# A routed expert layer: one loop for wide and narrow blocks, index products inside the down products

## The chip, the cores and the metric

The kernel runs on one core of a Trainium2 chip. The metric is the device time of one execution in microseconds (us). Engines: PE is TensorE (matrix products and transposes), DVE is VectorE, ACT is ScalarE, POOL is GpSimd, SP is SyncE. 16 DMA engines move data between the chip's memory (HBM) and the on-chip buffer.

## The reference

Two layers of a diffusion backbone over 512 latent and 256 context tokens of width 1024, in float32. Each layer has a mixer (recurrence and attention in the first, a state-space layer in the second) and then a routed mixture of 64 experts of hidden width 256 beside a shared one. Layer 0 routes all 768 tokens, layer 1 the 512 latent ones. What matters here is the expert part:

```python
def moe_ffn(h, router_w, router_bias, w_gate, w_up, w_down, ws_gate, ws_up, ws_down):
    affinity = jax.nn.sigmoid((h @ router_w).astype(f32))
    _, idx = lax.top_k(affinity + router_bias.astype(f32), TOP_K)      # TOP_K = 6
    ...
    def expert_block(acc, blk):
        tok, g, e = blk
        y = swiglu(h_ext[tok], w_gate[e], w_up[e], w_down[e])
        return acc.at[tok].add(y * g[:, None]), None
    ...
    return acc[:n_tok] + swiglu(h, ws_gate, ws_up, ws_down)
```

where `swiglu(x, g, u, d)` is `(silu(x @ g) * (x @ u)) @ d`. An expert's three matrices are 1 MB each (1024 x 256, 1024 x 256 and 256 x 1024).

## The kernel before

The program runs in order: preparation, mixer 0, the experts of layer 0, the state-space mixer, the experts of layer 1. An expert part is `moe_route` (router, ranks of the tokens, a table of work items), `moe_loop` and `moe_combine` (adds three accumulators in memory to the stream).

`moe_loop` is what changes. The tokens of an expert are cut into blocks. A **wide** block has up to 128 tokens on the 128 partitions. A **narrow** one has up to 64: each token lies as two half rows of 512 features on two partitions, and the products work on pairs of 64-column tiles. How many blocks of each kind there are is known only when the router has run, so each engine reads the counts from the table and walks loops of `UNROLL` = 6 unrolled bodies, each behind a branch (`items`, L1135 to L1140). First all wide blocks are done (`WIDE_TRIPS` trips of six: 72 counts in layer 0, 60 in layer 1), then all narrow ones (`NARROW_TRIPS`, 66 counts). A count beyond the number of blocks only costs the branch.

What a block takes, with its lines before the change:

- SP (`load`, L1148) reads the expert's number from the table, waits for `gu_mm` (gate and up products of the block whose ring slot is reused), issues the gate and up loads, waits for `y_mm` (that block's down products) and issues the down load. The wide ring has 2 slots, the narrow ring 3. SP works in order.
- DVE marks in `onehot` which tokens are in the block (`mark_wide`, `mark_narrow`), `AHEAD` = 4 blocks ahead. PE multiplies that with the table of ids and gates (`pick`, six small products in layer 0, L1340), DVE sums the result to indices and gates (`tokens`, L1289 to L1298), POOL gathers the rows (L1170, L1176).
- PE transposes the gathered rows into `pT` (L1347, L1353), ACT copies them to `xT`.
- PE multiplies gate and up (`up_wide` L1361, `up_narrow` L1372), ACT makes the silu (L1240, L1250), DVE the product `hid` (L1303, L1313), PE transposes it (L1383, L1404), DVE copies `hidT` (L1306, L1316), PE multiplies down (L1395, L1416), ACT copies the result with the gate as a scale (L1245, L1255), and POOL adds the rows to an accumulator in memory by an indirect DMA (L1186, L1196).

PE's order is written by hand: in the body of block i come gate and up of block i+1, then the hid transposes of i, the row transposes of i+2, `pick` of i+4, then the down products of i. So silu and product of a block lie beside other PE work. Each float32 product appears as two records.

## Time and profile before

| what | us |
|---|---|
| median of 3 runs | 3109.47 |
| lowest and highest of them | 3103.22, 3113.58 |
| the profiled execution | 3128.16 |
| its span, first to last instruction | 3126.4 |
| mean granted clock of PE, share of full speed | 0.857 |
| PE busy in the span | 2291.5 (73%) |
| weight loads of the experts, 3 x 138 of 1024 KB, median to landing | 10.2, 14.9, 13.1 |
| HBM read and written | 628.15 and 94.65 MB |

The first expert load of layer 0 is issued at 893.5 us, the last down product of its narrow blocks ends at 1779.4 and the combine begins at 1798.2. In layer 1 the same marks are 2345, 3075.7 and 3089.8. A DMA share is the mean busy share of the 16 DMA engines; q1 is SP's queue, q0 POOL's, which carries gathers and adds; the columns of a queue row are packets, MB and the time its packets took as a share of 16 engines over the window. A share can pass 1 a little where packets overlap. The number in brackets at the end of a timeline row is the idle time of that engine before the instruction and what ended it.

### The profile page before, as it was taken

The page shows a single profiled execution, that of the slowest core. Times are in us where ns is not written, and L with a number is a line of the kernel's source. Part 1 is how long each engine was busy: PE and PEld are TensorE (multiplying, and loading weights), DVE is VectorE, ACT ScalarE, POOL GpSimd, SP SyncE. Part 2 cuts the span into 40 slices and gives each one's busy share as a digit, 9 for nine tenths or more (in the row PEclk, how much of TensorE's full clock was granted, in tenths as well). Part 3 has the DMA queues.
Part 4 walks back from the last instruction along what each step waited for, and adds up shares of the span by engine and source line. Part 5 has one row for each costly group of instructions (what it writes and reads, how often), then busy time and mean ns, then how long its engine had stood idle before and what let it go on. Part 6 is the DMA issues. An engine that isn't in the chain of part 4 may idle for free. (4 is left out here: it accounts for less than half of the span.)

```text
span 3126.4 us, 40427 instructions
## 1 busy us (share of the span) xinstructions
PE 2291.5 (73%) x12118; PEld 1322.8 (42%) x12119; DVE 969.9 (31%) x2071; ACT 584.4 (19%) x964; POOL 566.7 (18%) x468
## 2 busy tenths in 40 slices
PE   3996996677758889887787606269776886777772
PEld 2884543443434444444444305265343443444441
DVE  4742256641411111111222147842231111111113
ACT  2232233420201111111111113021111111111110
POOL 2530000000011111122232231300002112222222
PEclk8998998969879999998999857558987898999986
DMA  9973101001337787788999575123136877999995
GB/s 321 337 261 114 54 27 67 1 1 56 157 141 251 262 283 245 275 274 323 397 387 376 208 250 167 32 91 114 44 128 237 277 240 284 395 375 367 383 380 170
DMA packets 183539, 684.02 MB, mean 219 GB/s; under 512 B 34234, under 2 KB 36730, under 8 KB 145082
## 3 DMA queue, kind: packets, MB, share of 16 engines
q1 hardware_dynamic: 136042, 581.86, 49.7%
q0 software_dynamic: 38784, 71.13, 9.6%
q10 hardware_dynamic: 8624, 29.82, 2.4%
q8 instruction: 58, 0.95, 0.1%
q14 instruction: 31, 0.25, 0.0%
HBM read 628.15 MB, written 94.65 MB: 231 GB/s over the span
## 5 line engine op out<-in xcount | busy, mean ns | idle before, releaser
L1372 PE MATMUL pGU_m<-wgu_m,xT_m 128*64 128x256 f32 x2816 | 376.5, 428 | 158.9 <-DMA wgu_m<-in_exp_w_up 158.9
L1361 PE MATMUL pGU_m<-wgu_m,xT_m 128*128 128x512 f32 x800 | 401.2, 660 | 85.9 <-DMA wgu_m<-in_exp_w_up 85.9
L1372 PEld LDWEIGHTS pGU_m<-wgu_m,xT_m 128*64 128x64 f32 x2816 | 221.5, 154 | 348.3 <-DMA wgu_m<-in_exp_w_up 228.7
L1361 PEld LDWEIGHTS pGU_m<-wgu_m,xT_m 128*128 128x128 f32 x800 | 168.0, 213 | 314.3 <-issue 208.6
L1176 POOL DMA_INDIRECT xgn_m<-moe_h,idxn_m x96 | 99.8, 1040 | 500.2 <-DVE idxn_m L1295 472.9
L1395 PE MATMUL pY_m<-wd_m,hidT_m 128*128 128x512 f32 x400 | 186.9, 610 | 0.1
L1416 PE MATMUL pY_m<-wd_m,hidT_m 128*64 128x512 f32 x704 | 173.7, 612 | 4.0
L1316 DVE COPY hidT_m<-pHT_m 128x128 f32<-128x128 f32 x88 | 25.6, 291 | 433.9 <-PE pHT_m L1404 433.9
L1196 POOL DMA_INDIRECT moe_acc<-yn_m,idxn_m x88 | 140.0, 1591 | 108.0 <-ACT yn_m L1255 99.9
L1231 ACT ACTIVATE xT_m<-pT_m 128x1024 f32<-128x1024 f32 x54 | 55.2, 1023 | 531.0 <-PE pT_m L1347 531.0
L1234 ACT ACTIVATE xT_m<-pT_m 128x512 f32<-128x512 f32 x92 | 54.9, 597 | 529.3 <-PE pT_m L1353 529.3
L819 POOL MEMSET zero_r<- 128x1024 f32 x2 | 1.9, 951 | 794.7 <-POOLq L69 523.7
L1170 POOL DMA_INDIRECT xgw_m<-moe_h,idxw_m x58 | 60.0, 1035 | 465.2 <-DVE idxw_m L1298 457.0
L1306 DVE COPY hidT_m<-pHT_m 128x256 f32<-128x256 f32 x50 | 21.2, 424 | 393.4 <-PE pHT_m L1383 393.4
L1283 DVE TENSOR_TENSOR onehot_m<-iota_slot_l,rank_l 128x512 bf16 (+1 forms) x96 | 77.6, 809 | 181.5 <-issue 181.5
L579 PE MATMUL ps_a<-W_a,hT_a 128*128 128x512 f32 x288 | 124.1, 592 | 0.0
L2186 PE MATMUL ps_s<-UV_s,ZU_s 128*128 128x512 f32 x256 | 113.1, 605 | 0.7 <-ACT ZU_s L2006 0.7
L2155 PE MATMUL ps_s<-XS_s,Wb_s 128*128 128x64 f32 x256 | 54.8, 421 | 77.6 <-ACT XS_s L1996 77.6
L1186 POOL DMA_INDIRECT moe_acc<-yw_m,idxw_m x50 | 79.6, 1592 | 161.4 <-ACT yw_m L1245 161.4
L1395 PEld LDWEIGHTS pY_m<-wd_m,hidT_m 128*128 128x128 f32 x400 | 73.0, 192 | 73.6 <-issue 73.4
L1340 PE MATMUL pI_m<-pick_rhs_l,onehot_m 128*128 x776 | 50.8, 168 | 54.9 <-DVE onehot_m L1276 31.9
L1276 DVE TENSOR_TENSOR onehot_m<-iota_slot_l,rank_l 128x768 bf16 (+1 forms) x58 | 50.3, 866 | 123.8 <-issue 123.8
(375 smaller groups left out, 3394.3 us busy)
## 6 DMA issues: line engine op xcount, KB each, us to landing
wgu_m<-in_exp_w_gate SPq DMA_DIRECT2D x138, 1024.0 KB, 10.2
wgu_m<-in_exp_w_up SPq DMA_DIRECT2D x138, 1024.0 KB, 14.9
wd_m<-in_exp_w_down SPq DMA_DIRECT2D x138, 1024.0 KB, 13.1
w_p<-in_mod_w SPq DMA_DIRECT2D x24, 2048.0 KB, 14.5
acc_c<-moe_acc SPq DMA_DIRECT2D x30, 512.0 KB, 11.1
W_a<-in_ar_w_in SPq DMA_DIRECT2D x5, 2048.0 KB, 8.5
moe_acc<-zero_r ACTq DMA_DIRECT2D x20, 512.0 KB, 18.0
s_w<-Wt_p ACTq DMA_DIRECT2D x8, 1152.0 KB, 9.8
```

The source lines that it names most:

```text
L579: last = pe.matmul(bank(n % 4), hT[:, k, t * P:(t + 1) * P], W[:, c % 2, k, :], start=(k == 0), stop=(k == KD - 1))
L1170: pool.indirect_dma_start(xg_w[b % 3][:], None, h_dram, bass.IndirectOffsetOnAxis(idx[0][b][:].bitcast(U32), 0), bounds_check=last_row, oo ...
L1176: pool.indirect_dma_start(xg_n[b % 3][:], None, h_half, bass.IndirectOffsetOnAxis(idx[1][b][:].bitcast(U32), 0), bounds_check=last_half, o ...
L1186: pool.indirect_dma_start(accs[b % 2], bass.IndirectOffsetOnAxis(idx[0][b][:].bitcast(U32), 0), y_w[b % 2][:], None, bounds_check=last_row ...
L1196: pool.indirect_dma_start(acc_half[b % 3], bass.IndirectOffsetOnAxis(idx[1][b][:].bitcast(U32), 0), y_n[b % 3][:], None, bounds_check=last ...
L1231: act.activation(xT[b][:], pT[:].rearrange("p (k c) -> p k c", c=P), ACT.Copy).then_inc(W['xT_done'], 1)
L1283: dve.tensor_tensor(onehot[:].rearrange("p t (a s) -> p t a s", a=2), slots, rank[:, :, bass.ds(e, 1)].rearrange("p t (a o) -> p t a o", a ...
L1361: last = pe.matmul(pGU[b % 2][:], xT[b % 2][:, k, :], wgu[b % WIDE_RING][:, :, k, :], start=(k == 0), stop=(k == KD - 1))
L1372: last = pe.matmul(pGU[b % 2][H * side:H * side + H, 0, :].rearrange("p (j n) -> p j n", j=2), narrow_xT[b % 2][:, k % 4, H * (k // 4):H * ...
L1395: last = pe.matmul(pY[:, half * 512:(half + 1) * 512], hidT[:, k, :], wd[b % WIDE_RING][:, k, half * 512:(half + 1) * 512], start=(k == 0) ...
L1416: last = pe.matmul(pY[H * side:H * side + H, (b % 2) * 512:(b % 2 + 1) * 512], hidT[:, 0, H * k:H * k + H], w[:, k, side * 512:(side + 1) ...
L2186: last = pe.matmul(ps[:, (2 * (u % 4) + half) * 512:(2 * (u % 4) + half + 1) * 512], zT[:, k, m * P:(m + 1) * P], glu[:, k, c:c + 512], st ...
```

## The change

- The two loops become one (`trips`). Each of its `TRIPS` (12 in layer 0, 11 in layer 1, six counts each) takes, per count i, up to four steps, each behind its own branch: wide gate and up of i, narrow gate and up of i, the rest of wide i, the rest of narrow i. When the wide blocks are used up, the narrow ones go on alone.
- SP issues the gate and up loads of both kinds, then the down loads of both kinds.
- PE's `pick` moves from before the down products to between their halves. The wide row transposes are split in two halves of four, with one bank of `pT_w`, and a half stands on either side of the first half of the down products. Gate and up of block i now stand in the body of block i itself.
- DVE's `mark` moves behind `tokens` and works one block further ahead, with a `onehot` of each kind. At the end of each rest PE waits for `idx_done`.
- Wide and narrow have their own tiles: one `pGU_w` bank, `pGU_n` with two halves, `hid`, `hidT`, `xT`, `pY` of each kind, and a shared bank for `pHT` and `pI`. `y_n` has 2 buffers instead of 3.
- Wide adds go to accumulator 0 alone, each after the one before has landed; narrow adds alternate between accumulators 1 and 2.
- Wide down weights are loaded as one row of 8 KB for each partition instead of two of 4 KB, and `hid`'s columns are transposed in the order that fits. Narrow down weights stay as they are.
- The prologue fills both kinds alternately. ACT follows the order silu wide, silu narrow, rest wide, rest narrow.

```diff
-    WIDE_TRIPS = -(-most_wide // UNROLL)
-    NARROW_TRIPS = -(-NE // UNROLL)
-    assert max(most_wide, NE) + AHEAD <= ROWS
+    TRIPS = -(-max(most_wide, NE) // UNROLL)
+    assert max(most_wide, NE) + AHEAD + 1 <= ROWS
...
-        def items(eng, n, trips, body):
-
-            with eng.Fori(0, trips) as q:
+        def trips(eng, n_wide, n_narrow, steps):
+
+            with eng.Fori(0, TRIPS) as q:
                 for b in range(UNROLL):
-                    with eng.If(n > q * UNROLL + b):
-                        body(q * UNROLL + b, q, b)
...
+                    i = q * UNROLL + b
+                    for kind, step in steps:
+                        with eng.If((n_narrow if kind else n_wide) > i):
+                            step(i, q, b)
 
         @block.sync
         def _(sp):
-            def load(kind, i, q, b):
-                ring = (WIDE_RING, NARROW_RING)[kind]
-                slot = b % ring
-                to = slot + WIDE_RING * kind
+            def gate_up(kind, i, b):
+                slot = b % (WIDE_RING, NARROW_RING)[kind]
                 e = expert(sp, kind, i)
                 sp.wait_ge(S[kind]['gu_mm'], i + 1)
                 for j, w in enumerate((w_gate, w_up)):
-                    sp.dma_start(wgu[to][:, j], w[bass.ds(e, 1)].rearrange("e (p k) n -> p (e k) n", k=KD))\
+                    sp.dma_start(wgu[kind][slot][:, j], w[bass.ds(e, 1)].rearrange("e (p k) n -> p (e k) n", k=KD))\
                       .then_inc(gu_loaded[kind][slot], 16)
+
+            def down(kind, i, b):
+                slot = b % (WIDE_RING, NARROW_RING)[kind]
+                e = expert(sp, kind, i)
                 sp.wait_ge(S[kind]['y_mm'], i + 1)
-                sp.dma_start(wd[to][:], w_down[bass.ds(e, 1)].rearrange("e (k p) n -> p (e k) n", p=P))\
+                rows = ("e (p k) n -> p (e k) n", "e (k p) n -> p (e k) n")[kind]
+                sp.dma_start(wd[kind][slot][:], w_down[bass.ds(e, 1)].rearrange(rows, k=2))\
                   .then_inc(d_loaded[kind][slot], 16)
-            items(sp, count(sp, 0), WIDE_TRIPS, lambda i, q, b: load(0, i, q, b))
-            items(sp, count(sp, 1), NARROW_TRIPS, lambda i, q, b: load(1, i, q, b))
+
+            trips(sp, count(sp, 0), count(sp, 1),
+                  ((0, lambda i, q, b: gate_up(0, i, b)), (1, lambda i, q, b: gate_up(1, i, b)),
+                   (0, lambda i, q, b: down(0, i, b)), (1, lambda i, q, b: down(1, i, b))))
...
             def wide(i, q, b):
                 pool.wait_ge(W['idx_done'], i + AHEAD + 1)
-                pool.wait_ge(W['xT_mm'], i + 2)
+                pool.wait_ge(W['xT_mm'], i * 2 + 4)
                 gather_wide((b + AHEAD) % UNROLL)
                 pool.wait_ge(W['y_done'], i + 2)
+                pool.wait_ge(yw_added, i * 16 + 32)
                 pool.sem_inc(W['pool_go'], 1)
-                pool.indirect_dma_start(accs[b % 2], bass.IndirectOffsetOnAxis(idx[0][b][:].bitcast(U32), 0),
+                pool.indirect_dma_start(accs[0], bass.IndirectOffsetOnAxis(idx[0][b][:].bitcast(U32), 0),
                                         y_w[b % 2][:], None, bounds_check=last_row, oob_is_err=False,
-                                        compute_op=ALU.add).then_inc(y_added[b % 2], 16)
+                                        compute_op=ALU.add).then_inc(yw_added, 16)
...
+            def rest_wide(i, q, b):
+                for half in range(2):
+                    act.wait_ge(W['xT_mm'], i * 2 + 5 + half)
+                    evac_wide(b, half)
+                act.wait_ge(W['y_mm'], i + 1 + WIDE_RING)
+                act.wait_ge(yw_added, i * 16 + 16)
+                act.activation(y_w[b % 2][:], pY_w[:], ACT.Copy, scale=gslot[0][b][:]).then_inc(W['y_done'], 1)
...
+            def gated_wide(i, q, b):
                 dve.wait_ge(W['silu_done'], i + 1)
-                dve.tensor_tensor(hid[:], hsil[:], pGU[b % 2][:, 1, :], ALU.mult).then_inc(W['hid_done'], 1)
+                dve.tensor_tensor(hid_w[:], hsil_w[:], pGU_w[:, 1, :], ALU.mult).then_inc(W['hid_done'], 1)
                 dve.wait_ge(W['hidT_mm'], i + 1)
                 dve.wait_ge(W['y_mm'], i + WIDE_RING)
-                dve.tensor_copy(hidT[:], pHT[:]).then_inc(W['hidT_done'], 1)
-                dve.wait_ge(y_added[b % 2], q * 48 + 16 * (b // 2) + 16)
+                dve.tensor_copy(hidT_w[:], pHT).then_inc(W['hidT_done'], 1)
+
+            def gated_narrow(i, q, b):
+                dve.wait_ge(N['silu_done'], i + 1)
+                dve.tensor_tensor(hid_n[:], hsil_n[:], pGU_n[:, b % 2, 1, :], ALU.mult).then_inc(N['hid_done'], 1)
+
+            def rest_wide(i, q, b):
+                dve.wait_ge(yw_added, i * 16 + 16)
                 tokens(0, i + AHEAD, (b + AHEAD) % UNROLL)
-
-            def narrow(i, q, b):
-                mark_narrow(i + AHEAD)
-                dve.wait_ge(N['silu_done'], i + 1)
-                dve.tensor_tensor(hid[:, 0:P], hsil[:, 0:P], pGU[b % 2][:, 0, P:2 * P], ALU.mult).then_inc(N['hid_done'], 1)
+                mark_wide(i + (AHEAD + 1))
+
+            def rest_narrow(i, q, b):
                 dve.wait_ge(N['hidT_mm'], i + 1)
                 dve.wait_ge(N['y_mm'], i + NARROW_RING)
-                dve.tensor_copy(hidT[:, 0], pHT[:, 0]).then_inc(N['hidT_done'], 1)
-                dve.wait_ge(y_added[(b + 1) % 3], wide_adds(nw, (b + 1) % 3) * 16 + q * 32 + 16 * ((b + 1) // 3) + 16)
+                dve.tensor_copy(hidT_n[:], pHT[:, 0, :]).then_inc(N['hidT_done'], 1)
+                dve.wait_ge(yn_added[b % 2], q * (16 * UNROLL // 2) + 16 * (b // 2) + 16)
                 tokens(1, i + AHEAD, (b + AHEAD) % UNROLL)
+                mark_narrow(i + (AHEAD + 1))
...
-            def wide(i, q, b):
-                with pe.If(n_wide > q * UNROLL + (b + 1)):
-                    up_wide((b + 1) % UNROLL, i + 2, q * (32 * UNROLL // WIDE_RING) + 32 * ((b + 1) // WIDE_RING + 1), i + 1)
+            def rest_wide(i, q, b):
                 pe.wait_ge(W['hid_done'], i + 2)
-                pe.wait_ge(W['hidT_done'], i + 1)
                 for k in range(2):
-                    last = pe.transpose(pHT[:, k, :], hid[:, k * P:(k + 1) * P], ident[:])
+                    last = pe.transpose(pHT[:, k, :], hid_w[:].rearrange("p (c k) -> p k c", k=2)[:, k, :], ident[:])
                 last.then_inc(W['hidT_mm'], 1)
                 pe.wait_ge(gathered[0][(b + 2) % 3], q * (16 * UNROLL // 3) + 16 * ((b + 2) // 3 + 1))
-                pe.wait_ge(W['xT_done'], i + 2)
-                rows_wide((b + 2) % UNROLL)
-                pe.wait_ge(W['idx_done'], i + AHEAD)
-                pick(0, i + AHEAD)
-                pe.wait_ge(W['hidT_done'], i + 2)
+                pe.wait_ge(W['xT_done'], i * 2 + 4)
+                rows_wide((b + 2) % UNROLL, 0)
+                pe.wait_ge(W['hidT_done'], i + 1)
                 pe.wait_ge(d_loaded[0][b % WIDE_RING], q * (16 * UNROLL // WIDE_RING) + 16 * (b // WIDE_RING + 1))
                 pe.wait_ge(W['y_done'], i + 1)
                 for half in range(2):
                     for k in range(2):
-                        last = pe.matmul(pY[:, half * 512:(half + 1) * 512], hidT[:, k, :],
-                                         wd[b % WIDE_RING][:, k, half * 512:(half + 1) * 512], start=(k == 0), stop=(k == 1))
+                        last = pe.matmul(pY_w[:, half * 512:(half + 1) * 512], hidT_w[:, k, :],
+                                         wd[0][b % WIDE_RING][:, k, half * 512:(half + 1) * 512], start=(k == 0), stop=(k == 1))
+                    if half == 0:
+                        pick(0, i + AHEAD)
+                        pe.wait_ge(W['xT_done'], i * 2 + 5)
+                        rows_wide((b + 2) % UNROLL, 1)
                 last.then_inc(W['y_mm'], 1)
-
-            def narrow(i, q, b):
-                with pe.If(n_narrow > q * UNROLL + (b + 1)):
-                    up_narrow((b + 1) % UNROLL, i + 2, q * (32 * UNROLL // NARROW_RING) + 32 * ((b + 1) // NARROW_RING + 1), i + 1)
+                pe.wait_ge(W['idx_done'], i + AHEAD + 1)
+
+            def rest_narrow(i, q, b):
                 pe.wait_ge(N['hid_done'], i + 2)
+                pe.transpose(pHT[:, 0, :], hid_n[:], ident[:]).then_inc(N['hidT_mm'], 1)
+                pe.wait_ge(gathered[1][(b + 2) % 3], q * (16 * UNROLL // 3) + 16 * ((b + 2) // 3 + 1))
+                pe.wait_ge(N['xT_done'], i + 2)
+                rows_narrow((b + 2) % UNROLL)
                 pe.wait_ge(N['hidT_done'], i + 1)
-                pe.transpose(pHT[:, 0, :], hid[:, 0:P], ident[:]).then_inc(N['hidT_mm'], 1)
-                pe.wait_ge(gathered[1][(b + 2) % 3], q * (16 * UNROLL // 3) + 16 * ((b + 2) // 3 + 1))
-                pe.wait_ge(N['xT_done'], i + 1)
-                rows_narrow((b + 2) % UNROLL)
-                pe.wait_ge(N['idx_done'], i + AHEAD)
-                pick(1, i + AHEAD)
-                pe.wait_ge(N['hidT_done'], i + 2)
                 pe.wait_ge(d_loaded[1][b % NARROW_RING], q * (16 * UNROLL // NARROW_RING) + 16 * (b // NARROW_RING + 1))
                 pe.wait_ge(N['y_done'], i + 1)
-                w = wd[WIDE_RING + b % NARROW_RING]
+                w = wd[1][b % NARROW_RING]
                 for k in range(2):
                     for side in range(2):
-                        last = pe.matmul(pY[H * side:H * side + H, (b % 2) * 512:(b % 2 + 1) * 512],
-                                         hidT[:, 0, H * k:H * k + H], w[:, k, side * 512:(side + 1) * 512],
-                                         start=(k == 0), stop=(k == 1))
+                        last = pe.matmul(pY_n[H * side:H * side + H, :], hidT_n[:, H * k:H * k + H],
+                                         w[:, k, side * 512:(side + 1) * 512], start=(k == 0), stop=(k == 1))
+                    if k == 0:
+                        pick(1, i + AHEAD)
                 last.then_inc(N['y_mm'], 1)
+                pe.wait_ge(N['idx_done'], i + AHEAD + 1)
...
+            trips(pe, n_wide, n_narrow, ((0, up_wide), (1, up_narrow), (0, rest_wide), (1, rest_narrow)))
```

Three places show the new order.

**SP, one trip's loads.** `wgu`, `wd` are the gate and up and the down weights; w and n at a name's end are wide and narrow. Before, in either loop:

```order
L1139 COMPARE_AND_BRANCH
...
L1133 TENSOR_LOAD table_l
...
L1155 DMA wgu_m<-in_exp_w_gate 128x2048
L1155 DMA wgu_m<-in_exp_w_up 128x2048
L1158 DMA wd_m<-in_exp_w_down 128x2x1024
```

and now, without the branch and the register load ahead of each pair:

```order
L1151 DMA wguw_m<-in_exp_w_gate 128x2048
L1151 DMA wguw_m<-in_exp_w_up 128x2048
...
L1151 DMA wgun_m<-in_exp_w_gate 128x2048
L1151 DMA wgun_m<-in_exp_w_up 128x2048
...
L1159 DMA wdw_m<-in_exp_w_down 128x2048
...
L1159 DMA wdn_m<-in_exp_w_down 128x2x1024
```

The gate and up loads of the narrow block moved ahead of the wide block's down load.

**PE, a wide body.** `pGU` holds gate and up, `pHT` (in `pHI` now) the transposed hidden values, `pT` the transposed rows, `pI` (in `pHI` now) the index products, `pY` the down products. Before:

```order
L1361 MATMUL pGU_m<-wgu_m,xT_m 128x512 x8
...
L1383 MATMUL pHT_m<-ident_l,hid_m 128x128 x2
...
L1347 MATMUL pT_m<-ident_l,xgw_m 128x128 x8
...
L1340 MATMUL pI_m<-pick_rhs_l,onehot_m 128x5
...
L1395 MATMUL pY_m<-wd_m,hidT_m 128x512 x4
```

and now one merged trip, up to the narrow transposes:

```order
L1369 MATMUL pGUw_m<-wguw_m,xTw_m 128x512 x8
...
L1380 MATMUL pGUn_m<-wgun_m,xTn_m 64x256 x16
...
L1388 MATMUL pHI_m<-ident_l,hidw_m 128x128 x2
...
L1355 MATMUL pTw_m<-ident_l,xgw_m 128x128 x4
...
L1398 MATMUL pYw_m<-wdw_m,hidTw_m 128x512 x2
...
L1348 MATMUL pHI_m<-pick_rhs_l,onehotw_m 128x5
...
L1355 MATMUL pTw_m<-ident_l,xgw_m 128x128 x4
L1398 MATMUL pYw_m<-wdw_m,hidTw_m 128x512 x2
...
L1409 MATMUL pHI_m<-ident_l,hidn_m 128x128
```

Between the hid transposes and the first down product stand four row transposes where eight and the index products stood.

**DVE, from the wide hid copy on.** Before, a wide body:

```order
L1276 TENSOR_TENSOR onehot_m<-iota_slot_l,rank_l 128x768
...
L1303 TENSOR_TENSOR hid_m<-hsil_m,pGU_m 128x256
...
L1306 COPY hidT_m<-pHT_m 128x256
...
L1290 TENSOR_REDUCE gslotw_m<-pI_m 128x1
L1291 TENSOR_REDUCE idf_m<-pI_m 128x1
L1298 TENSOR_SCALAR idxw_m<-idf_m 128x1
```

and now, wide and narrow:

```order
L1310 COPY hidTw_m<-pHI_m 128x256
...
L1314 TENSOR_TENSOR hidn_m<-hsiln_m,pGUn_m 128x128
...
L1295 TENSOR_REDUCE gslotw_m<-pHI_m 128x1
L1296 TENSOR_REDUCE idfw_m<-pHI_m 128x1
L1303 TENSOR_SCALAR idxw_m<-idfw_m 128x1
...
L1281 TENSOR_TENSOR onehotw_m<-iota_slot_l,rank_l 128x768
...
L1324 COPY hidTn_m<-pHI_m 128x128
```

The wide `onehot` and its register loads now stand ahead of the narrow `hidT` copy.

## Rows read from the trace of the kernel before

**Rows 1.** Page, part 2: GB/s of the DMA engines in 40 slices.
```profile
GB/s 321 337 261 114 54 27 67 1 1 56 157 141 251 262 283 245 275 274 323 397 387 376 208 250 167 32 91 114 44 128 237 277 240 284 395 375 367 383 380 170
```

**Rows 2.** Windows: us; busy PE, PEld, DVE, ACT, POOL; clock, DMA, GB/s.
```profile
930.00:1420.00 490.00, 428.31 (x1342) 208.66 (x1340) 72.90 (x200) 79.91 (x100) 86.46 (x66) 0.93 0.78 259
...
1480.00:1750.00 270.00, 209.06 (x1512) 114.30 (x1513) 57.54 (x180) 43.82 (x90) 79.09 (x60) 0.93 1.02 387
...
1779.40:1798.20 18.80, 0.03 (x1) 0.00 (x0) 0.00 (x0) 0.69 (x1) 1.59 (x1) 0.50 0.03 3
...
3075.70:3089.80 14.10, 0.00 (x0) 0.00 (x0) 0.00 (x0) 0.69 (x1) 1.59 (x1) 0.61 0.14 25
```

**Rows 3.** DMA queues, layer 0: wide 930 to 1420, narrow 1480 to 1750.
```profile
q1 hardware_dynamic: 18144, 102.37, 57.2%
...
q0 software_dynamic: 9250, 24.49, 20.7%
...
q1 hardware_dynamic: 17081, 95.68, 88.2%
...
q0 software_dynamic: 6637, 8.68, 13.4%
```

**Rows 4.** DMA queues, layer 1: wide 2380 to 2595, narrow 2660 to 3040.
```profile
q1 hardware_dynamic: 7840, 44.04, 56.1%
...
q0 software_dynamic: 4032, 8.79, 17.3%
...
q1 hardware_dynamic: 23669, 133.06, 87.6%
...
q0 software_dynamic: 9258, 11.39, 12.6%
```

**Rows 5.** Timeline, two wide blocks on PE: start, us, instruction, idle before.
```profile
1109.69 8.57 PE L1361 MATMUL pGU_m<-wgu_m,xT_m 128*128 128x512 f32 x16 [3.75 <-DMA wgu_m<-in_exp_w_up]
...
1118.32 1.13 PE L1347 MATMUL pT_m<-ident_l,xgw_m 128*128 128x128 f32 x8
...
1130.04 1.12 PE L1347 MATMUL pT_m<-ident_l,xgw_m 128*128 128x128 f32 x8
...
1131.15 3.68 PE L1395 MATMUL pY_m<-wd_m,hidT_m 128*128 128x512 f32 x8
```

**Rows 6.** Timeline, the row transposes of two narrow blocks on PE.
```profile
1455.24 0.65 PE L1353 MATMUL pT_m<-ident_l,xgn_m 128*128 128x128 f32 x4
...
1461.55 0.65 PE L1353 MATMUL pT_m<-ident_l,xgn_m 128*128 128x128 f32 x4
```

**Rows 7.** Timeline, DVE between two wide blocks.
```profile
1119.61 0.16 DVE L1290 TENSOR_REDUCE gslotw_m<-pI_m 128x1 f32<-128x3 f32 x1 [0.58 <-PE pI_m L1340]
...
1119.94 0.15 DVE L1298 TENSOR_SCALAR idxw_m<-idf_m 128x1 int32<-128x1 f32 x1
...
1121.67 0.96 DVE L1276 TENSOR_TENSOR onehot_m<-iota_slot_l,rank_l 128x768 bf16 x1 [1.58 <-issue]
```

**Rows 8.** Waits of the SyncE queue, 930 to 1420: total us, times, longest.
```profile
SPq L1158 <- PE pY_m L1395: 385.6, 32, 16.6
```

**Rows 9.** Lines, ACT, 900:1435, 1435:2000, 2374:2609, 2600:3126: xcount, busy, mean ns.
```profile
L1245 ACT ACTIVATE yw_m<-pY_m,gslotw_m 128x1024 f32<-128x1024 f32 x34 | 37.9, 1113 | 96.4 <-PE pY_m L1395 96.4
...
L1255 ACT ACTIVATE yn_m<-pY_m,gslotn_m 128x512 f32<-128x512 f32 x38 | 26.1, 687 | 66.4 <-PE pY_m L1416 66.4
...
L1240 ACT ACTIVATE hsil_m<-pGU_m 128x256 f32<-128x256 f32 x16 | 6.0, 375 | 6.7 <-PE pGU_m L1361 6.7
...
L1255 ACT ACTIVATE yn_m<-pY_m,gslotn_m 128x512 f32<-128x512 f32 x50 | 34.4, 687 | 83.9 <-PE pY_m L1416 83.9
```

**Rows 10.** Timeline, ACT: silu after each layer's first gate and up.
```profile
934.53 0.38 ACT L1240 ACTIVATE hsil_m<-pGU_m 128x256 f32<-128x256 f32 x1 [6.79 <-PE pGU_m L1361]
...
2381.90 0.38 ACT L1240 ACTIVATE hsil_m<-pGU_m 128x256 f32<-128x256 f32 x1 [6.68 <-PE pGU_m L1361]
```

**Rows 11.** Source L1139, the loop's branch on PE, 1781 to 1799.
```profile
L1139 PEldq COMPARE_BRANCH  x16: 208/208/208, 1781.0 to 1787.3; - x16
```

196 lines of the change are left out of this document (88 added, 108 removed).

## The prediction

> **What bounds the kernel now.** I read the slices of the page first [rows 1]. In the expert loop of layer 0 the DMA engines move 245 to 283 GB/s for about 500 us and then close to 390; layer 1 repeats this (237 to 284, then about 380). So each loop has two stages with different limits. The windows say which [rows 2]. In the wide stage (930 to 1420) PE is busy 428 of 490 us and the DMA share is 0.78. In the narrow stage (1480 to 1750) the DMA share is 1.02 and PE is busy 209 of 270 us. The first wants PE, the second wants DMA, and they run one after the other.
>
> The price of a block comes from the queue rows [rows 3, 4]. Three weight tiles are 3.146 MB, so 102.37 MB on q1 are 32.5 wide blocks in 490 us, 15.1 us each; 95.68 MB are 30.4 narrow blocks in 270 us, 8.9 us each. In layer 1: 14.0 in 215 us (15.4 each), 42.3 in 380 us (9.0 each). One wide and one narrow block cost 24.0 us one after the other in layer 0, 24.3 in layer 1.
>
> Why does a wide block take 15.1 us? From one set of row transposes to the next is 11.72 us where PE did not wait [rows 5]. The block before waited 3.75 us for weights and then needed 8.57 us for its gate and up products; the same in the undisturbed block is part of the 11.72. SyncE explains the wait: its queue stood 385.6 us of the stage before the load of the down weights, until PE was done with an older down product [rows 8], and the next gate and up loads stand behind that in order. Undisturbed, a narrow block takes 6.31 us of PE [rows 6].
>
> **The two resources of a merged trip.** DMA: I add the time shares of both queues at each kind's own price. Layer 0: wide (57.2% + 20.7%) x 490 / 32.5 = 11.74 us, narrow (88.2% + 13.4%) x 270 / 30.4 = 9.02 us. The saturated stage reaches a sum of 1.016, so a pair needs 20.76 / 1.016 = 20.4 us. Layer 1: 11.27 + 9.00 = 20.3, by its own sum of 1.00 20.2 us. The other bound is by bytes: 6.29 MB of weights, 0.754 MB of wide and 0.286 MB of narrow gathers and adds, 7.33 MB at the narrow stage's 387 GB/s, 18.9 us. I take the queue time, since a packet of the wide stage's gathers and adds was measured at its own duration, and keep 18.9 as the low end.
>
> The saturated row moved 387 GB/s. The Trainium skill, page "DMA: Bandwidth & Descriptors", section Specifications, gives a limit of about 358 GB/s of HBM for a core. The row is above it; by the page the 7.33 MB would take an estimated 20.5 us, by the row 18.9.
>
> PE: 11.72 + 6.31 = 18.0 us of work, plus three new exposures in the order. (a) The wide hidT copy is covered by four row transposes instead of eight and the index products: 0 to 0.5 us, I take 0.2. (b) In the narrow rest the hidT copy on DVE stands behind the wide index sums (0.48 us from the first to the last [rows 7]) and the wide onehot, which needs 1.58 us of register loads and 0.96 us of work; PE covers it by half the row transposes (0.56) and half the down product (1.84 [rows 5]) plus its own narrow transposes (0.65 [rows 6]): 0 to 1 us, I take 0.5. (c) After the narrow down product PE's sequencer waits for the narrow indices, with only the second half of that product queued behind it: 0.2 to 0.8 us, I take 0.5. Queued behind this wait is the next trip's whole gate and up product. Together 19.2 us, ends 18.2 to 20.3. PE is just under DMA, so I forecast DMA-bound trips of **20.4 and 20.2 us**.
>
> **Is DMA fed?** The moved loads on SyncE decide it. Now the gate and up loads of both kinds are issued once the wide product two trips back is done, and a down load no longer holds up its own kind's next gate and up load. When PE waits for a wide gate tile, behind it are queued the narrow one, two down tiles and the whole next trip, about 10 MB or 25 us. The queue does not run dry. The four loads a trip need four register loads and branches, hidden in 20 us. The single accumulator for wide adds makes each add wait for the one before, one trip of 20 us earlier; the narrow adds keep two. No cost.
>
> **Rows of 8 KB** change 128 descriptors of a wide down load. The 2 KB rows of the page's third slice reach 337 GB/s, the mixed 4 and 8 KB rows of the narrow stage 397 [rows 1]: 0.45 us per MB at most between them, so at most 0.2 us a wide block, at least 0. Within the rounding; 0 taken. The new hidden-column order costs no instruction.
>
> **Counts** are 34 wide and 38 narrow in layer 0, 16 and 50 in layer 1 [rows 9]. So 34 and 16 merged trips, then 4 and 34 trips with a narrow block alone. There, gate and up, silu, product and transposes stand in a row, where before the next block's product lay between. I estimate 1 to 2 us on top of 6.31 (the wide silu alone is 375 ns [rows 9]), so 7.3 to 8.3 us, still under the 8.9 to 9.0 of DMA: nothing taken, up to 1 us a trip kept for the range.
>
> **The end of the loop** gets dearer. 72 and 66 counts of the unrolled loop are walked whatever the blocks, and each now has four branches on PE. After layer 0's last narrow block 34 counts are left: 136 branches instead of 28. The rows show 16 of them in 6.3 us, 0.42 us each [rows 11]; part of that is loop and counter work that isn't multiplied, so 0.31 to 0.42, I take 0.37: 50 us, starting 3.7 us before the last product ends. Before, the combine began 18.8 us after it [rows 2]; now it would be 46.5: **28 us lost**. Layer 1: 64 branches, 24 us, about 21 against 14.1: **7 us lost**. The jump between the stages (38 and 44 branches) goes, but DMA was full there, so no gain counts.
>
> That branch took 208 ns itself. The Trainium skill, page "Advanced Engine Details and Errata", section Control Flow Timing, gives about 108 ns for compare-and-branch. The row is twice that; by the page the 136 branches would be an estimated 15 us, hidden before the combine, and both losses would be nil.
>
> **The sum.** Two pairs fit in the rings and load during the index work. The third pair's load starts when the first wide product ends: 934.5 and 2381.9 [rows 10]. Layer 0: 934.5 + 32 x 20.4 + 4 x 8.9 + 2 for the last down product = 1625, against 1779.4 before, 154 less; after the branches 126. Layer 1: 2381.9 + 14 x 20.2 + 34 x 9.0 + 2 = 2973 against 3075.7, 103 less; after the branches 96. Together 222 us. The profiled execution took 3128.2 us (span 3126.4), so 2906 in its terms; the median of the runs is 3109.5, so **2887**.
>
> **The rivals.** (1) *PE is the bound, and dearer than I think.* For it: PE is within 1.2 us of DMA, several waits now stand in one trip, and a wait for weights already cost 1.5 us in slower products. Against: the ends of the exposures sum to 20.3 only. At 22 us a trip: 32 x 1.6 + 14 x 1.8 = 76 more, 2963; with 1 us more for each of 38 narrow trips 3001. (2) *DMA is cheaper,* by bytes, and PE at 19.2 us is the floor: 32 x 1.2 + 14 x 1.0 = 52 less, 2835; with branches at 0.31 another 12 less, 2823. (3) *The clock turns it slower.* The granted clock is 0.93 in both stages [rows 2]; after a wait of 3.75 us the products took 8.57 us [rows 5]. If every piece of a merged trip, cut up by waits, ran at 1.2 instead of 2.4 GHz, PE would need up to 36 us. It decides from 222 / 46 = 4.8 us above my trip, 25.2 us, that is a third of PE's 18 us at the lower level. With half of it there a trip is 19.2 + 9 = 28.2: 46 x 7.9 = 363 more, 3250. Against: a trip has one wait for weights, of about 1 us. (4) *The loops don't overlap* because SyncE's order keeps DMA idle as now: 24 us a trip, then 46 x 3.7 = 170 more, 3057.
>
> For (3) the Trainium skill, page "TensorE: Matmul & The Clock Gate", section "HAM oscillation — how this bites in real kernels", says that a wait for DMA between short pieces of products can start every piece at the lower clock. By that rule each trip would start slow.
>
> **How the numbers follow.** Forecast 0.57, rival 1 0.20, rival 2 0.17, rival 3 0.03, rival 4 0.03. Differences under 0.3% (9 us) are what a measurement of this kernel can't tell from no change. The range 2825 to 2975 takes in rival 2 and most of rival 1; left out are its worst end, 3 and 4. Faster by over 0.3%: 0.96. Within: 0.01. Slower: 0.03.
>
> **What would show it.** Right: DMA share near 1.0 and about 360 to 380 GB/s through the whole loop; wide gate and up products 20 us apart, each after a wait of about 1 us for wgu; 4 then 34 narrow trips of 9 us; 136 branches of PE and some 45 us before layer 0's combine. Rival 1: DMA share under 0.95, PE's waits on DVE. Rival 3: granted clock under 0.8. Wrong altogether: a DMA share that still swings between 0.75 and 1.

## The result and the profile after

The changed kernel takes 2950.7 us (median of 4 runs, 2948.0 to 2961.0), the kernel before 3111.5 beside it. The ratio is 0.949, with a 95% interval of 0.9457 to 0.9523: 161 us gained where 222 were forecast. The profiled executions have spans of 2947.2 and 3126.4 us, 179 us apart.

Slices of the page of the kernel after, to be read beside [rows 1]: granted clock, DMA share and GB/s.

```profile
PEclk9998999879797999999999757557987999999996
DMA  9983100100509999999999274314035999999994
GB/s 321 353 292 129 57 29 0 72 1 0 211 36 357 347 363 349 367 353 355 357 354 327 77 241 156 80 48 170 0 154 229 378 357 353 364 335 392 391 382 145
```

The two stages of layer 0 have become one, with 347 to 367 GB/s and the DMA share above 0.9 (the last slice, in which the narrow-only trips begin, has 327). The windows of the kernel after (columns as in [rows 2]) are layer 0's merged trips, its four narrow-only trips, layer 1's merged and narrow-only trips, and the two stretches between the last down product and the combine:

```profile
930.00:1600.00 670.00, 631.09 (x2954) 315.16 (x2952) 129.95 (x394) 135.48 (x229) 172.08 (x130) 1.00 0.98 358
1621.00:1656.50 35.50, 29.43 (x204) 17.27 (x204) 7.91 (x24) 6.20 (x12) 10.56 (x8) 1.00 0.55 157
2285.00:2545.00 260.00, 247.40 (x1121) 122.06 (x1121) 44.64 (x156) 53.62 (x90) 68.38 (x52) 1.00 0.98 361
2560.00:2885.00 325.00, 271.83 (x1807) 155.14 (x1807) 63.44 (x222) 59.84 (x113) 98.08 (x74) 1.00 0.97 364
1656.50:1698.90 42.40, 0.12 (x2) 0.00 (x0) 0.96 (x1) 0.69 (x1) 2.64 (x2) 0.55 0.02 3
2890.20:2910.60 20.40, 0.07 (x2) 0.00 (x0) 0.69 (x1) 0.69 (x1) 2.63 (x2) 0.57 0.12 20
```

PE is busy 94% of the merged trips, and DMA's share is 0.98. Both look full. PE's waits in 930 to 1600 (us in total, times, the longest) say which of the two sets the trip:

```profile
PE pGUw_m L1369 <- issue: 14.4, 32, 0.8
PE pYn_m L1419 <- DVE hidTn_m L1324: 13.8, 32, 0.8
PE pYw_m L1398 <- DVE hidTw_m L1310: 10.2, 33, 0.3
```

No wait for weights stands there. PE waits for DVE, and for its own sequencer. Of the forecast's signs the DMA share and the GB/s came true and the wait of about 1 us for `wgu` did not; of rival 1's, the waits on DVE came and the share under 0.95 did not. So the shares alone would have confirmed the wrong bound. The length of a trip is read from the wide silu, which comes once a trip (ACT, layers 0 and 1, count, first and last start):

```profile
L1242 ACT ACTIVATE hsilw_m<-pGUw_m x34: 384/384/385, 926.1 to 1608.0; 128x256 f32<-128x256 f32 x34
...
L1242 ACT ACTIVATE hsilw_m<-pGUw_m x16: 384/384/385, 2280.8 to 2582.5; 128x256 f32<-128x256 f32 x16
```

That is 681.9 / 33 = 20.66 us a trip in layer 0 and 301.7 / 15 = 20.11 in layer 1. Here is one trip on PE (timeline: start, us, instruction, idle time before it):

```profile
1318.60 3.67 PE L1380 MATMUL pGUn_m<-wgun_m,xTn_m 128*64 128x256 f32 x32
1322.20 0.51 PE L1388 MATMUL pHI_m<-ident_l,hidw_m 128*128 128x128 f32 x2
...
1323.50 1.96 PE L1398 MATMUL pYw_m<-wdw_m,hidTw_m 128*128 128x512 f32 x4 [0.30 <-DVE hidTw_m L1310]
1325.30 0.29 PE L1348 MATMUL pHI_m<-pick_rhs_l,onehotw_m 128*128 x6
...
1328.94 1.08 PE L1419 MATMUL pYn_m<-wdn_m,hidTn_m 128*64 128x512 f32 x4 [0.46 <-DVE hidTn_m L1324]
1329.98 0.80 PE L1348 MATMUL pHI_m<-pick_rhs_l,onehotn_m 128*128 x6
...
1332.19 7.13 PE L1369 MATMUL pGUw_m<-wguw_m,xTw_m 128*128 128x512 f32 x16 [0.40 <-issue]
1339.25 3.03 PE L1380 MATMUL pGUn_m<-wgun_m,xTn_m 128*64 128x256 f32 x26
```

The reader sees three gaps (0.30, 0.46 and 0.40 us), and narrow index products that spread over 0.80 us where the wide ones take 0.29.

### The profile page after: what moved, and what is told of

It is laid out like the page before. It is cut to its first block and busy times, and to the rows that moved or that the text cites. A ratio compares the mean times of both kernels' runs of the same rounds, so it can differ in the third digit from the quotient of the medians.

```text
span 2947.2 us, 41851 instructions
## 1 busy us (share of the span) xinstructions
PE 2262.6 (77%) x12118; PEld 1306.1 (44%) x12119; DVE 965.4 (33%) x2075; ACT 602.9 (20%) x1018; POOL 569.8 (19%) x470
## 5 line engine op out<-in xcount | busy, mean ns | idle before, releaser
L1369 PE MATMUL pGUw_m<-wguw_m,xTw_m 128*128 128x512 f32 x800 | 358.6, 601 | 21.8 <-issue 21.8
L1380 PE MATMUL pGUn_m<-wgun_m,xTn_m 128*64 128x256 f32 x2816 | 323.3, 382 | 27.9 <-issue 27.9
L1380 PEld LDWEIGHTS pGUn_m<-wgun_m,xTn_m 128*64 128x64 f32 x2816 | 210.9, 137 | 171.7 <-issue 98.2
L1369 PEld LDWEIGHTS pGUw_m<-wguw_m,xTw_m 128*128 128x128 f32 x800 | 149.1, 191 | 232.7 <-issue 232.7
L1419 PE MATMUL pYn_m<-wdn_m,hidTn_m 128*64 128x512 f32 x704 | 189.9, 615 | 19.0 <-DVE hidTn_m L1324 16.6
L1398 PE MATMUL pYw_m<-wdw_m,hidTw_m 128*128 128x512 f32 x400 | 191.8, 602 | 15.5 <-DVE hidTw_m L1310 15.5
L1288 DVE TENSOR_TENSOR onehotn_m<-iota_slot_l,rank_l 128x512 bf16 (+1 forms) x98 | 79.3, 809 | 132.3 <-issue 132.3
L1233 ACT ACTIVATE xTw_m<-pTw_m 128x512 f32<-128x512 f32 x108 | 64.5, 597 | 205.2 <-PE pTw_m L1355 205.2
L1398 PEld LDWEIGHTS pYw_m<-wdw_m,hidTw_m 128*128 128x128 f32 x400 | 68.5, 191 | 71.3 <-issue 71.3
L1262 ACT ACTIVATE yn_m<-pYn_m,gslotn_m 128x512 f32<-128x512 f32 x88 | 60.5, 687 | 185.2 <-PE pYn_m L1419 175.1
L1242 ACT ACTIVATE hsilw_m<-pGUw_m 128x256 f32<-128x256 f32 x50 | 19.2, 384 | 345.3 <-PE pGUw_m L1369 345.3
```

The lines of the kernel that those rows point to most:

```text
L1233: act.activation(xT_w[b % 2][:, 4 * half:4 * half + 4, :], pT_w[:].rearrange("p (k c) -> p k c", c=P), ACT.Copy).then_inc(W['xT_done'], 1)
L1262: act.activation(y_n[b % 2][:], pY_n[:], ACT.Copy, scale=gslot[1][b][:]).then_inc(N['y_done'], 1)
L1288: dve.tensor_tensor(onehot[1][:].rearrange("p t (a s) -> p t a s", a=2), slots, rank[:, :, bass.ds(e, 1)].rearrange("p t (a o) -> p t a o" ...
L1369: last = pe.matmul(pGU_w[:], xT_w[b % 2][:, k, :], wgu[0][b % WIDE_RING][:, :, k, :], start=(k == 0), stop=(k == KD - 1))
L1380: last = pe.matmul(pGU_n[H * side:H * side + H, b % 2], xT_n[b % 2][:, k % 4, H * (k // 4):H * (k // 4) + H], w[:, :, k, P * side:P * side ...
L1398: last = pe.matmul(pY_w[:, half * 512:(half + 1) * 512], hidT_w[:, k, :], wd[0][b % WIDE_RING][:, k, half * 512:(half + 1) * 512], start=( ...
```

## The experiments

The theory after reading the trace: PE sets the trip, DMA is just hidden. The rival was the forecast itself: DMA sets it at 20.4 us. Beside that stood the question of what earned the gain: merging the loops, or the loads that moved on SyncE's queue.

### Half of the gate and up bytes

```diff
-  sp.dma_start(wgu[kind][slot][:, j], w[bass.ds(e, 1)].rearrange("e (p k) n -> p (e k) n", k=KD))
+  sp.dma_start(wgu[kind][slot][:, j, 0:4], w[...].rearrange("e (p k) n -> p (e k) n", k=KD)[:, 0:4])
```

> The kernel after, with only the first half (k 0 to 3) of every expert's gate and up weights loaded; the products of k 4 to 7 read the first half again, so PE has the same work and the results of the experts leave that half out. A merged trip moves 5.2 instead of 7.3 MB. Theory, PE is the bound after: a trip stays at 20.65 us, the DMA share of 930 to 1600 falls from 0.98 to about 0.7, and the time stays within 15 us of the kernel after (2951); the 34 narrow-only trips of layer 1 may fall a little below 8.9 us, if they too are bound by PE's chain. Rival, DMA is the bound and PE merely follows it (its share was 0.98): a trip falls to PE's own 19.2 us or less and the time by 50 times 1.45, about 70 us, to 2880.

The products of k 4 to 7 read the loaded half again, so PE's work stays the same. It took 2951.4 us (one execution), against 2950.7 of the kernel after. The windows of the merged trips and of layer 1's narrow-only trips in this run:

```profile
930.00:1600.00 670.00, 631.37 (x2963) 315.83 (x2959) 129.22 (x391) 134.64 (x228) 170.78 (x129) 1.00 0.82 256
...
2560.00:2885.00 325.00, 270.12 (x1809) 154.22 (x1808) 63.80 (x225) 58.95 (x113) 99.89 (x75) 1.00 0.83 256
```

Nearly a third of the bytes is gone and no time. DMA does not set the time of the kernel after anywhere in its loops, the narrow-only trips included. The DMA share fell only to 0.82, where bytes alone would give about 0.7: the share does not follow bytes (the edit also halves the rows of these loads, from 8 KB to 4 KB).

### Half of the wide gate and up products

```diff
-  for k in range(KD):
+  for k in range(KD // 2):
       last = pe.matmul(pGU_w[:], xT_w[b % 2][:, k, :], wgu[0][b % WIDE_RING][:, :, k, :], ...)
```

> The kernel after, with only the first four of the eight gate and up products of every wide block made (the other half of that sum is left out); all weights are still loaded. PE's trip is 3.5 us shorter, 17.1 us, and DMA has all its bytes. This measures the price of a merged trip on DMA by itself. Forecast's price by queue time: the trip is DMA-bound at 20.4 us and the whole gains at most 10 us on 2951. Price by bytes: 18.9 us a trip, 50 x 1.75 = 87 us less, about 2863. In both cases PE waits for weights in every trip, which it does not in the kernel after.

It took 2921.8 us (one execution), 29 less than the kernel after. The wide silus in layer 0, the first eight, the other 26, and all:

```profile
L1242 ACT ACTIVATE hsilw_m<-pGUw_m x8: 384/384/384, 929.5 to 1051.7; 128x256 f32<-128x256 f32 x8
...
L1242 ACT ACTIVATE hsilw_m<-pGUw_m x26: 384/384/385, 1076.0 to 1580.9; 128x256 f32<-128x256 f32 x26
...
L1242 ACT ACTIVATE hsilw_m<-pGUw_m x34: 384/384/385, 929.5 to 1580.9; 128x256 f32<-128x256 f32 x34
```

PE's longest wait in 930 to 1600, and the windows of the two parts:

```profile
PE pGUn_m L1380 <- DMA wgun_m<-in_exp_w_up: 58.1, 18, 5.1
...
930.00:1055.00 125.00, 111.71 (x577) 56.87 (x573) 28.18 (x85) 29.02 (x49) 36.92 (x28) 1.00 1.02 380
1070.00:1560.00 490.00, 413.22 (x2011) 209.11 (x2010) 96.84 (x292) 100.18 (x169) 131.42 (x99) 0.94 1.00 367
```

With 3.5 us less on PE the whole comes to 651.4 / 33 = 19.74 us a trip, but that average isn't DMA's price: it mixes two parts. The first seven trips take 122.2 / 7 = 17.5 us, close to PE's own 17.1, while the weights loaded ahead of the loop last. From there on PE waits for weights and DMA sets the trip: from 1051.7 to 1580.9 are 26 trips of 20.35 us, from 1076.0 on 25 of 20.2, at a DMA share of 1.00 and 367 GB/s. So a merged trip costs DMA 20.2 to 20.4 us. The forecast's price by queue time (20.4) was right and the one by bytes (18.9) too low, since the 387 GB/s that it assumes are not reached in these trips. The 29 us gained are, but for 2, the distance between DMA's end of layer 0's merged trips and PE's: the last wide silu comes at 1580.9 instead of 1608.0.

### The loads alone, in both kernels

The kernel after, with each kind's down load right behind its gate and up loads:

```diff
-  ((0, gate_up), (1, gate_up), (0, down), (1, down))
+  ((0, gate_up), (0, down), (1, gate_up), (1, down))
```

> The kernel after with SyncE's four loads of a trip in the order of the kernel before inside each kind: wide gate and up, wide down, narrow gate and up, narrow down. Theory: what the moved loads bring is that a down load, which waits for PE's down product two blocks back, no longer stands ahead of gate and up loads; in the merged trip there is a second block's work between them, so the queue is late by up to 5 us of a 20.65 us trip, and PE waits for the narrow gate tile for 0 to 2 us a trip: 0 to 100 us slower, I expect 30. Rival: with rings of two and 20 us a trip the order of the loads no longer matters, within 10 us of 2951.

It took 2954.6 us, ratio 0.948 (0.946 to 0.951): no difference to the kernel after that these runs can tell. The rival holds: PE waits for no weights, and a whole block of the other kind lies between. In the merged loop the order of the loads no longer matters. Then the kernel before, with the loops apart, and only SyncE's order changed:

```diff
-  gate_up(i); down(i)
+  gate_up(0)
+  ...
+      if n > i + 1: gate_up(i + 1)
+      down(i)
```

> The kernel before with one part of the change alone: SyncE issues the gate and up loads of block i+1 ahead of the down load of block i, the two loops stay apart. Theory, merging is what brings the time: the wide block falls from 15.1 us to its 11.7 us on PE or its 11.7 us of queue time, with 34 + 16 wide blocks at most 3.4 us each, 170 us, and since PE and DMA then meet within 0.1 us of each other, less: I expect 12.5 us a block, 130 us less than 3111, about 2980. That would be four fifths of what the whole change brought (161 us). Rival: the wide block stays near 15 us because the products that follow a wait run slower, not because of the order; then the time stays within 15 us of 3111 and the merging brought it all.

It took 2975.9 us, ratio 0.955 (0.9527 to 0.9574). A few lines of SyncE's program bring 139 us. Its windows over the wide and the narrow stage of layer 0:

```profile
935.00:1325.00 390.00, 387.94 (x1334) 196.59 (x1333) 72.85 (x202) 80.55 (x100) 86.76 (x66) 1.00 0.94 325
1345.00:1660.00 315.00, 252.56 (x1846) 141.09 (x1843) 67.55 (x212) 51.40 (x106) 92.48 (x70) 0.93 1.02 389
```

and its wide silu in layer 0:

```profile
L1252 ACT ACTIVATE hsil_m<-pGU_m x34: 373/375/383, 933.0 to 1320.8; 128x256 f32<-128x256 f32 x34
```

A wide block now takes 387.8 / 33 = 11.75 us, PE's own time, and a narrow one 8.78 (38 silus from 1348.6 to 1673.5). A pair is 20.5 us one after the other; the merged trip takes 20.66. So merging made no pair cheaper. What is left of its 25 us is the passage from the wide to the narrow loop, 28 us from silu to silu in each layer, and layer 0 gives that back in the walk over empty counts: the combine's first load of the sums is issued at 1697.8 in this run and at 1699.7 in the kernel after. The gain over this run is all in layer 1. Whether the kernel with its loops apart would gain as much from the later edits (`cover_pe`, `skip_empty`) was not run.

### Rows of 4 KB again

```diff
-  rows = ("e (p k) n -> p (e k) n", "e (k p) n -> p (e k) n")[kind]
+  rows = ("e (k p) n -> p (e k) n", "e (k p) n -> p (e k) n")[kind]
```

and the hidden columns transposed in two halves.

> The kernel after with the down weights of wide blocks in 4 KB rows again, and the hidden columns transposed in two halves as in the kernel before; all else stays. Theory: PE sets the trip, and the down loads have the time to be late: within 5 us of the kernel after (ratio to the kernel before 0.947 to 0.951). Rival: the rows carry part of the gain (a DMA share of 0.98 leaves 0.4 us a trip): over 10 us slower than the kernel after, and waits of PE for wd.

It took 2949.6 us, ratio 0.947 (0.945 to 0.949). The 8 KB rows bring nothing that can be measured here.

### The index products ahead of the down products

```diff
+  pick(0, i + AHEAD)
   for half in range(2):
       ...
       if half == 0:
-          pick(0, i + AHEAD)
```

and the same in the narrow block.

> The kernel after with each index product directly ahead of its down product instead of inside it. Theory by PE's waits in the kernel after (0.40 us between the narrow down product and the next wide gate product, 0.46 for the narrow hidT copy): the indices come 0.9 us earlier, so the wait for them after the narrow down product is gone, but in the wide block only half a down product (0.9 us) is left to cover the copy of the first four transposed rows: 0 to 0.4 us a trip less in one place, 0 to 0.3 more in the other, 20.3 to 20.7 us a trip, 0 to 20 us faster than the kernel after. Rival: the place inside the down product is what lets the indices be hidden; then a trip is over 0.5 us longer, 25 us slower or more.

It took 3131.6 us, ratio 1.005 (1.003 to 1.007): the whole gain is gone, and neither case had expected that size. PE in this run, from the wide hid transposes on:

```profile
1332.95 0.50 PE L1388 MATMUL pHI_m<-ident_l,hidw_m 128*128 128x128 f32 x2
1333.29 0.65 PE L1355 MATMUL pTw_m<-ident_l,xgw_m 128*128 128x128 f32 x4
1335.21 0.81 PE L1348 MATMUL pHI_m<-pick_rhs_l,onehotw_m 128*128 x6 [1.27 <-issue]
1335.88 3.03 PE L1399 MATMUL pYw_m<-wdw_m,hidTw_m 128*128 128x512 f32 x4
1338.70 1.06 PE L1355 MATMUL pTw_m<-ident_l,xgw_m 128*128 128x128 f32 x4
1339.55 2.13 PE L1399 MATMUL pYw_m<-wdw_m,hidTw_m 128*128 128x512 f32 x4
```

PE stands 1.27 us with no engine to wait for, and the half down product behind it takes 3.03 us instead of 1.96. The releaser "issue" is the clue: the index product needs the expert's number, which PE's sequencer loads into a register right ahead of it, and here the load stands behind the wait for hidT with nothing queued. So the same kernel again, the number loaded at the start of the block's rest (of the narrow block too):

```diff
   def rest_wide(i, q, b):
+      e = expert(pe, 0, i + AHEAD)
       pe.wait_ge(W['hid_done'], i + 2)
```

> The run pick_ahead with the expert's number loaded into PE's register at the start of a block's rest. In pick_ahead PE stood 1.14 and 1.27 us before its two index products of a trip with no engine to wait for, and 2.8 us a trip were lost. Theory: that is the register load and the waits ahead of it behind the wait for hidT, which the place inside the down product hides; with the load early the stall falls to 0.3 to 0.5 us, and a trip to 20.7 to 21.3 us: 2950 to 2980. Rival: the index product's own place (the indices, or the cover of the copy of the transposed rows) makes the loss: the time stays over 3080.

It took 2940.0 us, ratio 0.946 (0.944 to 0.948), 192 us less than without that line. The gap ahead of the same products in this run:

```profile
1320.18 0.81 PE L1348 MATMUL pHI_m<-pick_rhs_l,onehotw_m 128*128 x6 [0.51 <-DVE hidTw_m L1310]
1320.86 1.96 PE L1400 MATMUL pYw_m<-wdw_m,hidTw_m 128*128 128x512 f32 x4
```

So nearly the whole loss was the register load behind that wait: the place inside the down product serves mainly to hide it. Whether the place itself still matters isn't shown, since no run has the load early and the product inside with nothing else changed.

In layer 0 a trip of pick_ahead was (1705.4 - 932.3) / 33 = 23.4 us, 2.8 more than in the kernel after. Its two stalls (1.14 and 1.27 us, against 1.16 us of gaps in the kernel after) explain about 1.2 of them; the rest shows as slower products. In its narrow-only trips of layer 1 the down product behind the stall took 3.6 us, where the kernel after needs about 2.2; the granted clock there was 0.92 against 1.00:

```profile
2868.82 0.56 PE L1348 MATMUL pHI_m<-pick_rhs_l,onehotn_m 128*128 x4 [1.09 <-issue]
2869.31 3.57 PE L1420 MATMUL pYn_m<-wdn_m,hidTn_m 128*64 128x512 f32 x8
```

### PE's gaps covered

Three edits: the register load early (as above), the wait for the narrow indices moved behind the next narrow gate product, and on DVE the narrow hidT copy ahead of the wide onehot, which needs two more steps with their branches.

```diff
-  pe.wait_ge(N['idx_done'], i + AHEAD + 1)     # after the narrow down product
+  pe.wait_ge(N['idx_done'], i + AHEAD)         # after the next narrow gate product
...
-  (0, rest_wide), (1, rest_narrow)))           # DVE
+  (0, rest_wide), (1, hidT_narrow), (0, mark_wide), (1, rest_narrow)))
```

> The kernel after with three exposures of PE covered, the same products and bytes: the expert's number is loaded into PE's register at the start of a block's rest, not in front of its index product; the wait for the narrow indices stands behind the next narrow gate product; DVE copies the narrow hidT ahead of the wide onehot. Theory, PE is the bound and these 0.46 + 0.40 + 0.5 us a trip are its loss: PE needs 19.3 us, DMA, by the run with half of the products, 19.74, so a trip is 19.8 us and the time 50 x 0.85 = 42 us less than the kernel after, about 2909. Rival, forecast's DMA price: 20.4 us a trip, 12 us less. Third case: what is covered in one place is waited for in the next, within 9 us of 2951.

It took 2960.0 us, 9 more than the kernel after (the ratios, 0.9505 and 0.949, have intervals that overlap), though the merged trips came out as expected: wide silu from 927.6 to 1583.0, on average 19.86 us a trip, DMA share 1.00. The expected gain was lost in layer 1's narrow-only trips. DVE's waits there (2600 to 2880):

```profile
DVE hidn_m L1314 <- issue: 24.0, 4, 6.1
DVE hidTn_m L1323 <- PE pHI_m L1414: 15.2, 29, 0.7
DVE gslotn_m L1295 <- issue: 14.7, 4, 3.8
```

and a queue's row on the page of cover:

```profile
q14 instruction: 83, 0.68, 0.1%
```

DVE stands up to 6.1 us with its operands ready. In the kernel after the stretch has no such rows, and q14 has 33 packets. Two runs asked whether DVE's longer program is the cause: one without the DVE edit, and one that reaches it without more steps, by making the wide onehot after the wide product.

> The run cover without its change on DVE: the expert's number in PE's register ahead of time, and the wait for the narrow indices behind the next narrow gate product; DVE's order and its branches are those of the kernel after. In cover the 34 merged trips went as expected (19.86 us), but the 34 narrow-only trips of layer 1 lost it again: PE waited there up to 4.6 us for hid_n, DVE sat idle up to 6.1 us with no one to wait for, and 83 instead of 33 instruction packets came in on q14. Theory: the two further branches a count on DVE made its loop too long for what its instruction store holds, so code is fetched again in each trip through queues full of weights. Then here q14 has 33 packets again, a merged trip takes 19.9 to 20.2 us (the narrow hidT wait of 0.46 stays) and the time is 25 to 40 us under the kernel after: 2911 to 2926. Rival: the moved wait or PE's faster trips cause the stalls; then the time stays near 2955, with stalls in the narrow-only trips.

> As cover, but the wide onehot is made a trip's start earlier, between the wide product and the wait for hidT on DVE, where DVE waits 3.2 us a trip; that needs no further branch. Theory of the long loop: no stalls, q14 at 33 packets, a merged trip at DMA's 19.75 to 19.9 us, 2905 to 2915. Rival (PE's faster trips cause the stalls): near 2955 as cover. If the onehot then holds up the hidT copy (2.5 us of work in a gap of 3.2), PE's wait for hidTw of 0.30 us grows.

They took 2923.1 us (0.940, 0.938 to 0.942) and 2924.1 (0.941, 0.939 to 0.943). q14 has 33 and 32 packets, and in the narrow-only trips up to 2900 DVE waits for ACT, for PE and for the onehot's register loads only, as in the kernel after. So the two further steps on DVE cost what was lost; that their code is fetched again while the queues are full fits the 83 packets, but the fetches themselves were not followed.

The average trip of cover_pe, (1583.5 - 928.9) / 33 = 19.84 us, again has two parts. Its first 26 trips take 19.64 us on PE, 1.0 less than in the kernel after: the wait of 0.40 us is gone, and the narrow index products take 0.30 instead of 0.80. Its last seven take 20.6 and have the waits for weights. cover2 hides the narrow hidT copy (0.17 instead of 0.47 us), so its first 20 trips take 19.35 us, but its last twelve take 20.6, and it wins nothing over cover_pe. The last wide silu of half_products, cover, cover_pe and cover2 comes within 6 us (1577.3 to 1583.5) whatever PE's pace before: DMA sets this end.

### The empty counts skipped

```diff
+  more = smax(n_wide, n_narrow)
   with eng.Fori(0, TRIPS) as q:
+      with eng.If(more > q * UNROLL):
           for b in range(UNROLL):
```

> The kernel after with one branch ahead of each six counts of the unrolled loop, which passes over all 24 branches when no block of either kind is left. Theory: the 42.4 us from layer 0's last down product to the combine are the walk over 34 empty counts, 136 branches; 30 of these counts go for 5 branches, 120 x 0.31 = 37 us, and the work that then ends last on other engines (the last add, about 5 us) leaves 30 of them as gain; layer 1 has 22 counts left, of which 18 go: 22 us less of 20.4, so at most 14 down to the 6 us or so that the last add takes. Together 40 us less than the kernel after, about 2911. Rival: something else than branches (the last adds to memory, the barrier) fills the stretch: within 5 us of 2951.

It took 2918.0 us, ratio 0.937 (0.935 to 0.939), 33 less than the kernel after. The last narrow y, and then the combine's first loads in layer 0:

```profile
1661.51 0.69 ACT L1265 ACTIVATE yn_m<-pYn_m,gslotn_m 128x512 f32<-128x512 f32 x1 [2.41 <-PE pYn_m L1422]
...
1672.79 0.81 SPq L1471 DMA_DIRECT2D g_c<-modrow  x2
```

They lie 11.3 us apart; in the kernel after it was 42. The walk over the branches was that stretch, and PE's walk above all. The loop branch in the kernel after, on three engines, 1656 to 1699 (count, shortest, median and longest in ns, first and last start):

```profile
L1141 PEldq COMPARE_BRANCH  x137: 169/202/208, 1656.2 to 1697.4; - x137
L1141 ACTq COMPARE_BRANCH  x136: 45/45/45, 1656.8 to 1681.2; - x136
L1141 DVEq COMPARE_BRANCH  x136: 56/56/56, 1657.7 to 1687.8; - x136
```

A branch takes 202 ns on PE's sequencer and 45 and 56 on those of ACT and DVE, so PE's end comes last, after 0.30 us a branch with the work around it.

The loop itself ran 5 us later than in the kernel after. Layer 1 gave 4 instead of up to 14 us. The expectation had counted 22 empty counts there; 66 - 50 is 16 (the kernel after walks 64 branches), of which 12 go. Its last y and the combine's loads are still 15 us apart, although PE's last branch starts at 2871.7 and the combine only at 2880.8; what fills those 9 us isn't shown.

### Both together

The edits of cover_pe and skip_empty.

> The edits of cover_pe and of skip_empty together. cover_pe was 28 us, skip_empty 33 us under the kernel after; the one shortens merged trips, the other what follows the last block, so they should add: 2951 - 28 - 33 = 2890, with 5 us to either side (ratio to the kernel before 0.928 to 0.931). A merged trip stays at 19.8 us, DMA share 0.99 to 1.00, and about 10 us lie between layer 0's last down product and the combine. Rival: with the last trips shorter, the last adds on POOL and DMA take the place of the branches; then 2900 or more.

It took 2893.6 us (6 runs, 2888.5 to 2894.6), ratio 0.929 (0.927 to 0.932). That is 57 us where the two alone had brought 28 and 33: they add up nearly in full. This version is 216 us faster than the kernel before.

## Why the prediction was right and wrong

**The place of the time** was in the forecast's range, but through the mechanism of its first rival at a smaller price. That the wrong bound cost so little is luck: PE's trip came to lie just above DMA's. In the terms of its sum, on the profiled executions, the gain was 179 where 222 were forecast; the 43 us are accounted for below.

**The bound.** The step that failed is "PE is just under DMA, so I forecast DMA-bound trips". Forecast were 19.2 on PE and 20.4 on DMA; measured are 20.66 on PE (20.11 in layer 1) and 20.2 to 20.4 on DMA (half_products, once the weights loaded ahead are used up). DMA's term was right; PE's was 1.5 us too small, and that alone turned the order of the two. The trip came out 0.26 us longer than forecast.

**PE's exposures.** (a) 0.30 for 0.2, (b) 0.46 for 0.5, (c) 0.40 for 0.5: rightly sized from the rows. Missing was what no wait names. The narrow index products take 0.80 us instead of 0.29 because the register load ahead of them is no longer covered (0.30 in cover_pe, which loads it early); and what is left of the 2.65 us above 18.0, about 1 us, lies in the pieces themselves: the wide gate and up product spans 7.06 us (6.86 in before_loads_ahead), and the rests of both blocks are cut in more parts than the 11.72 and 6.31 us of [rows 5, 6] had.

**The start.** "Two pairs fit in the rings and load during the index work" gave the loop 32 trips to wait for. That credit is DMA's; with PE as the bound all 34 trips are its own. From the first wide silu at 926.1 to the last down product at 1656.5 are 730.4 us, forecast 690.4: 8.4 for the longer trips, 20.7 for one trip more, 10.9 for the rest of the last trip behind its silu. The silu itself came 8.4 us earlier than [rows 10], so layer 0 ends 31.5 us later than forecast. In layer 1 the 15 trips take 301.7 us where 14 took 282.8, and it ends 16.5 later. Those are the 48 us, less 5 from the tails. This was the largest term that was mis-sized, and it hangs wholly on which resource is the bound. For DMA the credit was right: with PE's work cut (half_products) the last wide silu comes at 1580.9, where the sum gives 934.5 + 32 x 20.4 = 1587 for the end of the last pair's loads.

**Is DMA fed?** The conclusion was right: no wait for weights in the merged trips. The reason was half right. "The moved loads on SyncE decide it" holds for the loops apart, where before_loads_ahead shows that the down load ahead of the gate loads [rows 8] was what made a wide block cost 15.1 us. In the merged loop it does not hold: loads_in_turn puts the down loads back and loses nothing that can be measured. Either part alone brings most of the gain: 139 us the order without the rest of the change, 160 the rest without the order. Rival 4 had priced "the loops don't overlap" at 24 us a pair; serial with the loads ahead it is 20.5.

**Narrow-only trips.** Forecast 7.3 to 8.3 us of PE under 8.9 of DMA. The kernel after has 8.9 (35.5 / 4) with a DMA share of 0.55 and 8.4 to 9.1, on average 8.7, in layer 1, and half_loads leaves them as they are: PE's chain is the bound. Its rows, with the silu and product in line:

```profile
2699.81 3.67 PE L1380 MATMUL pGUn_m<-wgun_m,xTn_m 128*64 128x256 f32 x32 [0.63 <-issue]
2704.25 0.33 PE L1409 MATMUL pHI_m<-ident_l,hidn_m 128*128 128x128 f32 x1 [0.77 <-DVE hidn_m L1314]
...
2706.25 0.57 PE L1348 MATMUL pHI_m<-pick_rhs_l,onehotn_m 128*128 x4
```

The estimate of 1 to 2 us above 6.31 left out the 0.63 to 1.0 us of waiting and branches ahead of the next product. It cost nothing in the sum, because both bounds lie near 8.9: in cover_pe, with the waiting ahead of the product gone, PE waits for weights instead, 25 times in these trips and 34.4 us in all.

**The end of the loop.** Forecast 46.5 and 21 us, measured 42.4 and 20.4. The branch's 208 ns in [rows 11] were the right ground. The 0.37 us a branch were 0.30, and the walk began 0.3 us ahead of the product's end instead of 3.7; the two errors offset each other in part. The 108 ns of the Trainium skill, page "Advanced Engine Details and Errata", section Control Flow Timing, would have hidden the walk; the trace has 202 ns on PE, and skip_empty shows that the walk was not hidden.

**8 KB rows.** Forecast 0; rows_4k is 1 us from the kernel after, below what these runs can tell apart. **The clock** (rival 3) went the other way: 1.00 in the merged loop, 0.93 before. The rule of the Trainium skill, page "TensorE: Matmul & The Clock Gate", section "HAM oscillation — how this bites in real kernels", did not bite in the kernel after, whose waits are 0.3 to 0.5 us. Its example waits 3 to 5 us for DMA before each piece, so the prediction's "each trip would start slow", with a wait of about 1 us, did not follow from it. Shorter waits did slow PE in pick_ahead: it stood 1.1 to 1.3 us twice a trip, the mean granted clock was 0.94 in layer 0's merged trips, and the half down product behind the stall took 3.03 us instead of 1.96.

## What to carry to other kernels

Before two loops are merged so that one's compute covers the other's transfers, look at what stands ahead of the late transfer on its queue: here a few lines that put the next block's loads ahead of a waiting one brought 139 of 161 us, and in the merged loop they were worth nothing more. If two resources come out within 10% of each other, work the sum out for both as the bound, the start and the end too, since a credit such as preloaded pairs belongs to one of them alone. For the same reason read a resource's price from the part of a stage in which it is waited for: the average over the whole stage of half_products, 19.74 us, would have made DMA look 0.6 us cheaper than it is. In an order written by hand, count a register load as an instruction that needs cover: behind a wait with an empty engine it cost more than the whole change had won.

## What was unexpected of the hardware

- A DMA share of 0.98 was not the bound: with nearly a third fewer bytes it read 0.82 and the time stayed the same. A merged trip's real price on DMA, 20.2 to 20.4 us at 367 GB/s, was only seen with work taken from PE, and the sum of the queues' time shares before the change had given it.
- The narrow-only trips moved up to 392 GB/s, merged trips, with gathers and adds of whole rows, no more than 368 over a stage, both at a share of about 1.
- One register load in front of a product with nothing queued was a stall of 1.1 to 1.3 us with its wait, and the products right behind it took 3.03 us instead of 1.96, and 3.6 instead of about 2.2.
- Two more steps with branches on DVE went with 83 packets on the instruction queue q14 instead of 33, and with single stalls of up to 6.1 us while the DMA engines were full.
- The same branch took 202 ns on PE's sequencer, 56 on DVE's and 45 on ACT's.
